# Attention units 3 to 6 of a two-block float32 forward pass: the wide product in halves

## The chip, the cores and the metric

One core of one Trainium2 chip runs the whole kernel. The metric is the device time in microseconds (us) of that core. TensorE multiplies (PE in the profile, its weight loads PEld), VectorE is DVE, ScalarE is ACT, GpSimd is POOL, and SyncE (SP) issues the weight DMAs.

## What is computed

The reference is a forward pass over 256 tokens of width 1024, in float32. The first block is two macaron layers (SwiGLU, gated linear attention or retention, SwiGLU, layer norms between them). The second block is one layer with three attention branches. The change stands in the second block's first projection, of which this matters here:

```python
proj = jnp.einsum('bsd,dc->bsc', x, w_in[layer])
(qa, ka, va, qi, ki, wi, qf, kf, vf, fg, qs, ks_, vs, gates) = jnp.split(proj, split_at, axis=-1)
o_a = _dsa_attention(heads(qa), heads(ka), heads(va),
                     qi.reshape(b, s, IDX_HEADS, IDX_DIM), ki, wi, slopes)
log_f = jax.nn.log_sigmoid((fg + b_forget[layer]).astype(jnp.float32))
o_b = _forgetting_attention(heads(qf), heads(kf), heads(vf), log_f)
o_c = _stick_breaking_attention(heads(qs), heads(ks_), heads(vs))
```

The first branch (`_dsa_attention`) scores every earlier token with 16 small index heads (`relu(qi . ki)` weighted by `wi`), keeps the 64 best keys of each query, and takes a softmax over these alone. The second adds the running sum of `log_f` to its logits.

## The kernel before

**Precision.** Every operand of a large product is split into a high part that TensorE's fast float32 format holds and a low part, the rest. A product is hi by hi, hi by lo and lo by hi, summed in PSUM. Weights come as tiles of 128x2048, one DMA each, in a ring of three slots (`RING = 3`). For tile m, ACT copies the high part (`split_hi`, L428) after the last use of tile m-3; DVE subtracts to get the low part (`split_lo`, L905); the DMA of tile m+3 waits for that subtraction.

**Units.** The second block's projection runs in units of 512 output columns, two weight tiles each. With n the first tile, unit u takes tiles n+2u and n+2u+1. Unit 0 gives the first branch's values, units 1 and 2 the index queries, 3 and 4 the first branch's queries and keys, 5 and 6 the second branch's, 7 its values, 8 and 9 the third branch's queries and keys, 10 its values. A unit's result goes to one of two pairs of PSUM banks, `pairs[0]` and `pairs[1]`. Semaphore `pair_free` counts how often a pair has been read out, `pair_count(u)` is the value that unit u brings it to, `ret_count` the same in an earlier stage. The other four banks, `acc`, take the small products of the attention itself.

**Three forms of a unit.** `tokens_unit` has the weights as the moving operand. `features_unit` has them as the stationary one: for each of 8 chunks of 128 rows and 4 blocks of 128 columns it issues three 256-column matmuls (`three`, L1574, L1577, L1578). One ACT copy (`part`, L678) reads the pair out, and the next unit writes the other pair meanwhile. `features_halves` (L1706, L1713) does two of the four blocks at a time. A 512-column matmul takes the high weights against the high and low activations side by side, and a 256-column one the low weights against the high activations. Half 0 goes through both tiles into one pair, half 1 again through both tiles into the other. Each pair then holds two parts, which have to be added: ACT copies one out (`against_lo_half`, L519) and DVE adds the other (`halves`, through `sum_half`, L997), which frees the pair. Half 0 signals `half_ready`; the tiles are released by half 1, the first one three quarters through the unit. In `before` the units 1, 2, 8 and 9 are halves, 3 to 6 are plain.

**Order.** Each engine's queue is written out by hand and runs in that order. `between={c: f}` puts small work f into TensorE's stream: ahead of chunk c in the plain forms; in the halves form the key is 2*(2*half + tile) ahead of the wide matmuls, and one more ahead of the narrow ones. The small work here is: `dots(p)`, index scores of pass p, whose relu is ACT's `relu_dots(p)` (L694) and whose weighting is DVE's `index_scores(p)` (L1297, L1299); `forget_sums`; `logits(0, g)`; `turn_p`, transposes of the probabilities (L2143 to L2145), copied out by `pt_copy` on ACT and DVE; `softmax_values`. On DVE, `pick_largest(tb, 4)` takes four rounds of eight maxima (L1307, L1308); four calls make up the choice of keys. `logits(0, g)` on DVE adds distances and takes row maxima (L1316 to L1330). `first_logits` on TensorE is `logits(0, 0)`; `third_logits` is `logits(0, 2)`, which waits for the row maxima of group 0 (`max_ready`), because it writes the same banks. After the exponentials (ACT, L707) and reciprocals (DVE, L1341), POOL scales the probabilities (L401) and `turn_p(0, ...)` waits for its last group.

Of the kernel before, what the change touches and what calls it, by code (L numbers as in the profile page):

```python
# [29 lines left out]
HEADS, HEAD_DIM = 8, 64  # L30
# [31 lines left out]
def build(nc, io):  # L62
    ctx = ExitStack()
    with ctx:
# [202 lines left out]

        wide = ["ffn0", "ffn1", "ffn2", "ret1", "ret2", "ret3", "ret4", "ffn3", "sec1", "sec2", "sec8", "sec9"]  # L270
        half_value = lambda what: wide.index(what) + 1
        copies_of = lambda what: 1 if what.startswith("ffn") else 2
        copied_value = lambda what, half: sum(copies_of(w) for w in wide[:wide.index(what)]) + half + 1
        ret_count = lambda u: 6 + u // 2
        pair_count = lambda u: 12 if u == 0 else (13 if u < 8 else 14) + u // 2

        block = ctx.enter_context(nc.Block())

# [129 lines left out]
        def _(act):  # L408
# [144 lines left out]
            n = N_GLA  # L553
# [118 lines left out]
            def part(u, out, scale=1.0, mid=None):  # L672

                split_hi(n + 2 * u + 3)
                if mid:
                    mid()
                act.wait_ge(weights_used, n + 2 * u + 2)
                nc.scalar.activation(out, pairs[u % 2], ACT.Copy, scale=scale).then_inc(pair_free[u % 2], 1)  # L678
# [11 lines left out]
            def relu_dots(p):  # L690
                act.wait_ge(dots_ready, p + 1)
                if p >= 2:
                    act.wait_ge(dots_used, p - 1)
                nc.scalar.activation(relu[:, p % 2, :].rearrange("p (b c) -> p b c", b=2),  # L694
                                     acc[:, 2 * (p % 2):2 * (p % 2) + 2, :], ACT.Relu).then_inc(relu_done, 1)
# [86 lines left out]
            halves(2, (pairs[1], pairs[0]), a_qi[:, 4:8, :], mid=lambda: relu_dots(0), late=lambda: relu_dots(1))  # L782
            split_hi(n + 8)
            relu_dots(2)
            part(3, as_pair(a_q[:, 0]), HEAD_DIM ** -0.5, mid=lambda: (relu_dots(3), relu_dots(4)))
            split_hi(n + 10)
            relu_dots(5)
            part(4, as_pair(a_k[:, 0]), mid=copy_sums)
            split_hi(n + 12)
            part(5, as_pair(a_q[:, 1]), HEAD_DIM ** -0.5)  # L790
            split_hi(n + 14)
            part(6, as_pair(a_k[:, 1]))
            split_hi(n + 16)
            softmax_exp(0, 0)
            part(7, a_v[:, 1], mid=lambda: softmax_exp(0, 1))
# [92 lines left out]
        def _(dve):  # L888
# [10 lines left out]
            def split_lo(n, i=0):  # L899

                if n >= N_TILES:
                    return
                s = slot_of(n)
                dve.wait_ge(hi_split, i * RING + (n + 1))
                nc.vector.tensor_tensor(w_lo[:, s, :], raw[:, s, :], w_hi[:, s, :].bitcast(F32),  # L905
                                        ALU.subtract).then_inc(lo_split, 1)
# [396 lines left out]
            def pick_largest(tb, rounds):  # L1303

                score = a_sc[:, 0, block_cols(tb)]
                for _ in range(rounds):
                    link(nc.vector.max(out=a_top[:, :], in_=score))  # L1307
                    link(nc.vector.match_replace(out=score, in_to_replace=a_top[:, :], in_values=score, imm_value=TAKEN))  # L1308
# [106 lines left out]
            for tb in range(TB):  # L1415
# [8 lines left out]
            index_scores(1)  # L1424
            split_lo(n + 8)
            index_scores(2)
            split_lo(n + 9)
            index_scores(3)
            index_scores(4)
            split_lo(n + 10)  # L1430
            index_scores(5)
            link(nc.vector.tensor_tensor(a_sc[:, 0, :], a_sc[:, 0, :], causal, ALU.add))
            dve.wait_ge(cT_copied, 1)
            nc.vector.scalar_tensor_tensor(out=a_cT[:, 1, :], in0=acc[0:HEAD_DIM + HEADS, 0, 0:TOK], scalar=-1.0,
                                           in1=a_cT[:, 0, :].bitcast(F32), op0=ALU.mult, op1=ALU.subtract).then_inc(cT_split, 1)
            split_lo(n + 11)
            pick_largest(1, 4)
            split_lo(n + 12)
            pick_largest(1, 4)
            split_lo(n + 13)  # L1440
            pick_largest(0, 4)
            split_lo(n + 14)
            pick_largest(0, 4)

            link(nc.vector.tensor_scalar(a_sc[:, 0, :], a_sc[:, 0, :], TAKEN, NEG, ALU.not_equal, ALU.mult))
            link(nc.vector.tensor_tensor(a_sc[:, 0, :], a_sc[:, 0, :], causal, ALU.min))
            split_lo(n + 15)
            logits(0, 0)
            split_lo(n + 16)
            logits(0, 1)  # L1450
# [116 lines left out]
        def _(pe):  # L1567
# [495 lines left out]
            def unit(u, kind, **between):  # L2063
                await_pair(u)
                kind(n + 2 * u, pairs[u % 2], **between)
# [160 lines left out]
            pe.wait_ge(wf_copied, 1)  # L2226
            pe.wait_ge(ki_doubled, 16)
            features_halves(n + 4, (pairs[1], pairs[0]), awaits(1, 12, 0, 13), "sec2", between={4: lambda: dots(0), 6: lambda: dots(1)})
            unit(3, features_unit, between={1: lambda: dots(2), 3: lambda: dots(3), 5: lambda: dots(4)})
            unit(4, features_unit, between={1: lambda: dots(5), 4: forget_sums})  # L2230
            unit(5, features_unit)

            def first_logits():
                pe.wait_ge(pick_copied, 1)
# [12 lines left out]
            def third_sums():  # L2247
                pe.wait_ge(max_ready, 3 + 1)
                key_sums(2)

            unit(6, features_unit, between={4: first_logits, 6: lambda: logits(0, 1)})
            unit(7, tokens_unit, between={4: third_logits})
            features_halves(n + 16, pairs, awaits(0, 16, 1, 16), "sec8")
            turn_p(0, range(0, 4))
            features_halves(n + 18, pairs, awaits(0, 17, 1, 17), "sec9", between={4: lambda: turn_p(0, range(4, 8))})
            unit(10, tokens_unit, between={0: lambda: softmax_values(0, 0), 2: lambda: softmax_values(0, 1),
                                           3: lambda: key_sums(0), 4: lambda: logits(1, 0), 5: second_sums,
                                           6: lambda: logits(1, 1)})
            merge_unit(0, between={1: third_sums, 2: lambda: logits(1, 2)})
# [176 lines left out]
```

## Time and profile before

| | us |
|---|---|
| median of 3 runs (1535.52 to 1535.70) | 1535.62 |
| the profiled execution's own time | 1535.63 |
| its span in the trace | 1533.8 |
| PE busy | 1525.2 |
| DVE busy | 966.8 |
| ACT busy | 754.6 |
| POOL busy | 130.8 |

1.83 us of the profiled execution lie outside the span. Busy time of PE overstates it: the records of matmuls overlap, so start-to-start times are the ones to read. The units 3 to 8 begin at 1094.67, 1110.03, 1124.11, 1135.63, 1149.71 and 1161.82 us of the span, unit 8 ends at 1172.97. In the timeline view the first column is the start, the second the duration (from the first start to the last end where a row merges several), in brackets the idle time ahead of it and what ended it.

### The profile page before, as it was taken

The numbers are of one execution on the slowest core, as the hardware profiler recorded it, in microseconds if no ns is written. First come the engines' busy times: TensorE is split into PE (matmuls) and PEld (weight loads), VectorE is DVE, ScalarE is ACT, GpSimd is POOL, SyncE is SP. The second block draws the span as 40 slices with busy tenths as digits, with TensorE's granted clock in tenths as the row PEclk, the third lists the DMA queues.
The fourth block names the chain that finished last, engine by engine and source line by source line (L and its number), as shares of the span: only waits on it lengthen the run. The fifth ranks groups of instructions, "written<-read, shape, count | busy, mean of one in ns | idle before, by whom it ended". The sixth has DMA issues, their size and how long they took to land.

```text
span 1533.8 us, 20565 instructions
## 1 busy us (share of the span) xinstructions
PE 1525.2 (99%) x8204; PEld 1301.6 (85%) x8204; DVE 966.8 (63%) x983; ACT 754.6 (49%) x723; POOL 130.8 (9%) x141
## 2 busy tenths in 40 slices
PE   9999999999999999999999999999999999999998
PEld 8888888788888888888878888888898788888886
DVE  6555676665557655577557665657686556775565
ACT  5454455554454545454335445445536556354442
POOL 1000020110002000024021200002002200020000
PEclk9999999999999999999999999999999999999999
DMA  7545564355544654556444465455444444455551
GB/s 308 196 189 184 198 220 165 110 220 195 193 187 165 234 200 169 200 211 220 172 165 162 149 238 192 168 215 215 173 155 148 144 159 165 165 197 202 193 188 71
DMA packets 42264, 283.71 MB, mean 185 GB/s; under 512 B 5088, under 2 KB 5536, under 8 KB 9552
## 3 DMA queue, kind: packets, MB, share of 16 engines
q1 hardware_dynamic: 38016, 270.55, 48.3%
q0 software_dynamic: 2368, 8.59, 1.6%
q10 hardware_dynamic: 1808, 3.55, 0.6%
q8 instruction: 54, 0.88, 0.2%
q14 instruction: 18, 0.15, 0.0%
HBM read 281.55 MB, written 1.05 MB: 184 GB/s over the span
## 4 chain that ended last, share of the span: by engine, by line
PE 99%; DVE 0%; ACT 0%; DVEq 0%; POOLq 0%; issue 0%; POOL 0%; ACTq 0%
PE psum L1679 20%; PE psum L1574 16%; PE psum L1577 16%; PE psum L1578 16%; PE psum L1683 11%; PE psum L1706 5%; PE psum L1713 2%; PE psum L1619 2%; PE psum L1606 2%; PE psum L1612 2%; PE psum L1586 1%; PE psum L2004 1%; PE psum L2133 0%; PE psum L2096 0%; PE psum L2154 0%; PE psum L1830 0%
## 5 line engine op out<-in xcount | busy, mean ns | idle before, releaser
L905 DVE TENSOR_TENSOR weights_lo<-weights_raw,weights_hi 128x2048 fp32r<-128x2048 f32 x247 | 569.7, 2318 | 324.6 <-ACT weights_hi L428 323.4
L428 ACT ACTIVATE weights_hi<-weights_raw 128x2048 fp32r<-128x2048 f32 (+1 forms) x254 | 479.5, 1890 | 297.0 <-PE psum L1578 140.3
L1679 PE MATMUL psum<-operand,weights_hi 128*128 128x512 f32 x1376 | 327.6, 390 | 0.0
L1679 PEld LDWEIGHTS psum<-operand,weights_hi 128*128 128x128 f32 x1376 | 255.3, 188 | 51.1
L1574 PE MATMUL psum<-weights_hi,hidden_hi 128*128 128x512 f32 x480 | 187.7, 391 | 0.0
L1577 PE MATMUL psum<-weights_lo,hidden_hi 128*128 128x512 f32 x480 | 187.6, 391 | 0.0
L1578 PE MATMUL psum<-weights_hi,hidden_lo 128*128 128x512 f32 x480 | 186.8, 389 | 0.0
L1683 PEld LDWEIGHTS psum<-operand,weights_lo 128*128 128x128 f32 x1376 | 176.4, 191 | 6.7
L1683 PE MATMUL psum<-operand,weights_lo 128*128 128x256 f32 x1376 | 178.5, 283 | 0.0
L1574 PE MATMUL psum<-weights_hi,operand 128*128 128x512 f32 x384 | 153.4, 399 | 0.0
L1577 PE MATMUL psum<-weights_lo,operand 128*128 128x512 f32 x384 | 150.0, 391 | 0.0
L1578 PE MATMUL psum<-weights_hi,operand 128*128 128x512 f32 x352 | 137.3, 390 | 0.0
L1578 PEld LDWEIGHTS psum<-weights_hi,hidden_lo 128*128 128x128 f32 x480 | 90.1, 188 | 19.0
L1574 PEld LDWEIGHTS psum<-weights_hi,hidden_hi 128*128 128x128 f32 x480 | 90.3, 188 | 17.5
L1577 PEld LDWEIGHTS psum<-weights_lo,hidden_hi 128*128 128x128 f32 x480 | 90.3, 188 | 17.0
L499 ACT ACTIVATE gate_up<-psum 128x512 f32<-128x512 f32 x72 | 39.1, 595 | 129.0 <-PE psum L1683 129.0
L322 POOL TENSOR_SCALAR ln_rstd<-variance 128x1 f32<-128x1 f32 x16 | 5.1, 317 | 1015.3 <-ACTq L450 1015.3
L1036 DVE TENSOR_TENSOR gate_up<-psum,gate_up 128x512 f32<-128x512 f32 x72 | 46.4, 687 | 68.0 <-ACT gate_up L499 68.0
L1574 PEld LDWEIGHTS psum<-weights_hi,operand 128*128 128x128 f32 x384 | 72.1, 188 | 17.5 <-issue 2.8
L1577 PEld LDWEIGHTS psum<-weights_lo,operand 128*128 128x128 f32 x384 | 72.2, 188 | 14.2 <-issue 0.5
L1706 PE MATMUL psum<-operand,weights_hi 128*128 128x512 f32 x320 | 80.5, 393 | 0.0
L1578 PEld LDWEIGHTS psum<-weights_hi,operand 128*128 128x128 f32 x352 | 66.1, 188 | 14.1
(295 smaller groups left out, 1836.1 us busy)
## 6 DMA issues: line engine op xcount, KB each, us to landing
weights_raw<-in_weights SPq DMA_DIRECT2D x254, 1024.0 KB, 4.8
ln_rows<-in_ln_rows POOLq DMA_DIRECT2D x16, 512.0 KB, 6.7
weights_raw<-in_weights SPq DMA_DIRECT2D x4, 512.0 KB, 6.6
normalised<-in_x SPq DMA_DIRECT2D x2, 512.0 KB, 6.2
ret_constants<-in_ret_constants ACTq DMA_DIRECT2D x1, 1024.0 KB, 7.4
out<-normalised SPq DMA_DIRECT2D x4, 256.0 KB, 2.0
gla_w_low<-in_gla_w_low ACTq DMA_DIRECT2D x1, 512.0 KB, 5.5
att_w_small<-in_att_w_small ACTq DMA_DIRECT2D x1, 512.0 KB, 5.6
```

The source lines that it names most:

```text
L428: nc.scalar.activation(w_hi[:, s, whole], raw[:, s, whole], ACT.Copy).then_inc(hi_split, 1)
L499: nc.scalar.activation(gate_up[:, at:at + 2, :], against_lo(banks), ACT.Copy).then_inc(against_lo_copied, 1)
L905: nc.vector.tensor_tensor(w_lo[:, s, :], raw[:, s, :], w_hi[:, s, :].bitcast(F32), ALU.subtract).then_inc(lo_split, 1)
L1036: nc.vector.tensor_tensor(gate_up[:, at:at + 2, :], against_hi(banks), gate_up[:, at:at + 2, :], ALU.add).then_inc(up_summed if at else ga ...
L1574: mm(out, a_hi, b_hi, start=start, stop=False, skip_group_check=True)
L1577: mm(out, a_hi, b_lo, start=False, stop=False, skip_group_check=True)
L1578: return mm(out, a_lo, b_hi, start=False, stop=stop, skip_group_check=True)
L1606: mm(out[:, tb, :], x_hi[:, c, t], w_hi[:, slot, cols], start=c == 0, stop=False, skip_group_check=True)
L1612: ins = mm(out[:, tb, :], x_lo[:, c, t], w_hi[:, slot, cols], start=False, stop=last and c == KC - 1, skip_group_check=True)
L1679: mm(banks[b // 2][:, b % 2, :], w_hi[:, slot, cols], x_both[:, c, :, :].rearrange("p a t -> p (a t)"), start=c == 0, stop=False, skip_gro ...
L1683: last = mm(banks[b // 2][:, b % 2, 0:TOK], w_lo[:, slot, cols], x_hi[:, c, :], start=False, stop=c == KC - 1, skip_group_check=True)
L1706: mm(banks[half][:, b, :], w_hi[:, slot, cols], x_both[:, c, :, :].rearrange("p a t -> p (a t)"), start=c == 0, stop=False, skip_group_che ...
```

## The change

Units 3 to 6 take the halves form. They enter the list `wide`, and `pair_count` rises by two from unit 1 on, as each halves unit reads out both pairs. On TensorE their small work keeps its keys. `sec8` and `sec9` wait for higher counts. The first `turn_p` moves from between units 8 and 9 into unit 9, key 2 (half 0, second tile); the second from key 4 to key 6 (half 1, second tile); the first `softmax_values` from chunk 0 to chunk 1 of unit 10. On ACT `part` becomes `halves`: two copies of 512 columns in the place of one of 1024, the first as soon as half 0 is done. On DVE eight additions (L997) come in, put among the splits, `index_scores` and `pick_largest`; and `split_lo(n + 11)` now stands ahead of `index_scores(5)`, the other splits two steps apart as before.

```diff
-        wide = [..., "ffn3", "sec1", "sec2", "sec8", "sec9"]
+        wide = [..., "ffn3", "sec1", "sec2", "sec3", "sec4", "sec5", "sec6", "sec8", "sec9"]
-        pair_count = lambda u: 12 if u == 0 else (13 if u < 8 else 14) + u // 2
+        pair_count = lambda u: 12 if u == 0 else (15 if u < 8 else 16) + u // 2
...
-            part(3, as_pair(a_q[:, 0]), HEAD_DIM ** -0.5, mid=lambda: (relu_dots(3), relu_dots(4)))
+            halves(3, (pairs[1], pairs[0]), a_q[:, 0], HEAD_DIM ** -0.5, mid=lambda: relu_dots(3), late=lambda: relu_dots(4))
             split_hi(n + 10)
             relu_dots(5)
-            part(4, as_pair(a_k[:, 0]), mid=copy_sums)
+            halves(4, (pairs[1], pairs[0]), a_k[:, 0], mid=copy_sums)
             split_hi(n + 12)
-            part(5, as_pair(a_q[:, 1]), HEAD_DIM ** -0.5)
+            halves(5, (pairs[1], pairs[0]), a_q[:, 1], HEAD_DIM ** -0.5)
             split_hi(n + 14)
-            part(6, as_pair(a_k[:, 1]))
+            halves(6, (pairs[1], pairs[0]), a_k[:, 1])
...
             index_scores(2)
+            halves(3, 0, a_q[:, 0], HEAD_DIM ** -0.5)
             split_lo(n + 9)
             index_scores(3)
+            halves(3, 1, a_q[:, 0], HEAD_DIM ** -0.5)
+            split_lo(n + 10)
             index_scores(4)
-            split_lo(n + 10)
+            halves(4, 0, a_k[:, 0])
+            split_lo(n + 11)
             index_scores(5)
...
-            split_lo(n + 11)
-            pick_largest(1, 4)
+            halves(4, 1, a_k[:, 0])
             split_lo(n + 12)
             pick_largest(1, 4)
+            halves(5, 0, a_q[:, 1], HEAD_DIM ** -0.5)
             split_lo(n + 13)
-            pick_largest(0, 4)
+            pick_largest(1, 4)
+            halves(5, 1, a_q[:, 1], HEAD_DIM ** -0.5)
             split_lo(n + 14)
             pick_largest(0, 4)
-
+            halves(6, 0, a_k[:, 1])
+            split_lo(n + 15)
+            pick_largest(0, 4)
             link(nc.vector.tensor_scalar(a_sc[:, 0, :], a_sc[:, 0, :], TAKEN, NEG, ALU.not_equal, ALU.mult))
             link(nc.vector.tensor_tensor(a_sc[:, 0, :], a_sc[:, 0, :], causal, ALU.min))
-            split_lo(n + 15)
+            halves(6, 1, a_k[:, 1])
             logits(0, 0)
...
-            unit(3, features_unit, between={1: lambda: dots(2), 3: lambda: dots(3), 5: lambda: dots(4)})
-            unit(4, features_unit, between={1: lambda: dots(5), 4: forget_sums})
-            unit(5, features_unit)
+            features_halves(n + 6, (pairs[1], pairs[0]), awaits(1, 13, 0, 14), "sec3", between={1: lambda: dots(2), 3: lambda: dots(3), 5: lambda: dots(4)})
+            features_halves(n + 8, (pairs[1], pairs[0]), awaits(1, 14, 0, 15), "sec4", between={1: lambda: dots(5), 4: forget_sums})
+            features_halves(n + 10, (pairs[1], pairs[0]), awaits(1, 15, 0, 16), "sec5")
...
-            unit(6, features_unit, between={4: first_logits, 6: lambda: logits(0, 1)})
+            features_halves(n + 12, (pairs[1], pairs[0]), awaits(1, 16, 0, 17), "sec6", between={4: first_logits, 6: lambda: logits(0, 1)})
             unit(7, tokens_unit, between={4: third_logits})
-            features_halves(n + 16, pairs, awaits(0, 16, 1, 16), "sec8")
-            turn_p(0, range(0, 4))
-            features_halves(n + 18, pairs, awaits(0, 17, 1, 17), "sec9", between={4: lambda: turn_p(0, range(4, 8))})
-            unit(10, tokens_unit, between={0: lambda: softmax_values(0, 0), 2: lambda: softmax_values(0, 1),
+            features_halves(n + 16, pairs, awaits(0, 18, 1, 18), "sec8")
+            features_halves(n + 18, pairs, awaits(0, 19, 1, 19), "sec9", between={2: lambda: turn_p(0, range(0, 4)), 6: lambda: turn_p(0, range(4, 8))})
+            unit(10, tokens_unit, between={1: lambda: softmax_values(0, 0), 2: lambda: softmax_values(0, 1),
```

## Rows read from the trace of the kernel before

**Rows 1.** The page: span, busy times, and the chain that ended last, by engine.

```profile
PE 1525.2 (99%) x8204; PEld 1301.6 (85%) x8204; DVE 966.8 (63%) x983; ACT 754.6 (49%) x723; POOL 130.8 (9%) x141
...
PE 99%; DVE 0%; ACT 0%; DVEq 0%; POOLq 0%; issue 0%; POOL 0%; ACTq 0%
```

**Rows 2.** The waits view, PE's only row: waiter, releaser, total, times, longest.

```profile
PE psum L1830 <- DVE squares L1059: 1.4, 1, 1.4
```

**Rows 3.** Stretches: length; PE, PEld, DVE, ACT, POOL busy; granted PE clock, DMA share.

```profile
0.00:1.45 1.45, 0.00 (x1) 0.00 (x1) 0.48 (x1) 0.26 (x1) 0.29 (x5) 1.00 0.00 0
...
1094.67:1110.03 15.36, 15.36 (x131) 14.09 (x130) 12.54 (x21) 7.17 (x6) 0.00 (x0) 1.00 0.45 155
1110.03:1124.11 14.08, 14.08 (x126) 13.82 (x126) 11.41 (x22) 5.99 (x6) 0.00 (x0) 1.00 0.37 138
1124.11:1135.63 11.52, 11.52 (x98) 11.52 (x98) 10.01 (x21) 4.74 (x3) 0.00 (x0) 1.00 0.44 173
1135.63:1149.71 14.08, 14.08 (x114) 13.06 (x114) 13.11 (x39) 4.74 (x3) 0.00 (x0) 1.00 0.55 176
...
1161.82:1172.97 11.15, 11.15 (x66) 9.83 (x65) 6.66 (x25) 8.31 (x20) 7.45 (x14) 1.00 0.49 182
```

**Rows 4.** Timeline of PE: halves in unit 2; third logits in unit 7.

```profile
1080.95 2.00 PE L1706 MATMUL psum<-operand,weights_hi 128*128 128x512 f32 x8
1082.79 1.12 PE L1713 MATMUL psum<-operand,weights_lo 128*128 128x256 f32 x8
1083.75 2.00 PE L1706 MATMUL psum<-operand,weights_hi 128*128 128x512 f32 x8
...
1155.15 1.16 PE L2133 MATMUL psum<-att_kT,att_qT 64*128 64x128 f32 x16
```

**Rows 5.** Timeline of ACT: a split and a copy-out, both in unit 1's half 1.

```profile
1078.42 1.92 ACT L428 ACTIVATE weights_hi<-weights_raw 128x2048 fp32r<-128x2048 f32 x1 [2.58 <-PE psum L1713]
1081.15 0.60 ACT L519 ACTIVATE att_qiT<-psum 128x512 f32<-128x512 f32 x1 [0.82 <-PE psum L1713]
```

**Rows 6.** Timeline of DVE: the work that stands between units 4 and 7.

```profile
1080.37 2.29 DVE L905 TENSOR_TENSOR weights_lo<-weights_raw,weights_hi 128x2048 fp32r<-128x2048 f32 x1 [3.62 <-ACT weights_hi L428]
...
1095.50 0.69 DVE L997 SCALAR_TENSOR_TENSOR att_qiT<-psum,att_qiT 128x512 f32<-128x512 f32 x1 [0.39 <-ACT att_qiT L519]
1096.10 2.04 DVE L1299 SCALAR_TENSOR_TENSOR att_score<-att_pT,att_wi_fg,att_score 128x256 f32<-128x256 f32 x4
...
1115.24 3.06 DVE L1299 SCALAR_TENSOR_TENSOR att_score<-att_pT,att_wi_fg,att_score 128x128 f32<-128x128 f32 x8
1118.45 0.56 DVE L1432 TENSOR_TENSOR att_score<-att_score,att_constants 128x384 f32<-128x384 f32 x1
1119.64 0.42 DVE L1434 SCALAR_TENSOR_TENSOR att_minus_cT<-psum,att_minus_cT 72x256 fp32r<-72x256 f32 x1 [0.64 <-ACT att_minus_cT L700]
...
1129.38 0.42 DVE L1307 MAX8 att_top<-att_score 128x8 f32<-128x256 f32 x1
...
1133.31 2.29 DVE L905 TENSOR_TENSOR weights_lo<-weights_raw,weights_hi 128x2048 fp32r<-128x2048 f32 x1
...
1140.90 0.29 DVE L1307 MAX8 att_top<-att_score 128x8 f32<-128x128 f32 x1
...
1143.76 0.36 DVE L1445 TENSOR_SCALAR att_score<-att_score 128x384 f32<-128x384 f32 x1
...
1144.75 2.29 DVE L905 TENSOR_TENSOR weights_lo<-weights_raw,weights_hi 128x2048 fp32r<-128x2048 f32 x1
...
1149.92 0.17 DVE L1330 TENSOR_SCALAR att_max<-att_max 128x4 f32<-128x4 f32 x1
1152.65 2.29 DVE L905 TENSOR_TENSOR weights_lo<-weights_raw,weights_hi 128x2048 fp32r<-128x2048 f32 x1 [2.56 <-ACT weights_hi L428]
```

**Rows 7.** Timeline of POOL: scaling of the first branch's probabilities, three groups.

```profile
1158.18 4.35 POOL L401 TENSOR_SCALAR att_p<-att_p,att_sum 128x256 f32<-128x256 f32 x4 [91.90 <-DVE att_sum L1341]
1164.86 6.73 POOL L401 TENSOR_SCALAR att_p<-att_p,att_sum 128x256 f32<-128x256 f32 x12 [2.33 <-DVE att_sum L1341]
```

More of the change, by code:

```diff
@@ L266, in build @@
         sig_of = lambda half, b: sig[3 if (half, b) == (1, 2) else b]
-        wide = ["ffn0", "ffn1", "ffn2", "ret1", "ret2", "ret3", "ret4", "ffn3", "sec1", "sec2", "sec8", "sec9"]
+        wide = ["ffn0", "ffn1", "ffn2", "ret1", "ret2", "ret3", "ret4", "ffn3", "sec1", "sec2", "sec3", "sec4", "sec5", "sec6", "sec8", "sec9"]
         half_value = lambda what: wide.index(what) + 1
@@ L1435, in _ @@
                                            in1=a_cT[:, 0, :].bitcast(F32), op0=ALU.mult, op1=ALU.subtract).then_inc(cT_split, 1)
-            split_lo(n + 11)
-            pick_largest(1, 4)
+            halves(4, 1, a_k[:, 0])
             split_lo(n + 12)
             pick_largest(1, 4)
+            halves(5, 0, a_q[:, 1], HEAD_DIM ** -0.5)
             split_lo(n + 13)
+            pick_largest(1, 4)
+            halves(5, 1, a_q[:, 1], HEAD_DIM ** -0.5)
+            split_lo(n + 14)
             pick_largest(0, 4)
-            split_lo(n + 14)
+            halves(6, 0, a_k[:, 1])
+            split_lo(n + 15)
             pick_largest(0, 4)
```

## The prediction

> **What bounds the kernel now.** The page comes first: PE is busy for 99% of the span and the chain that ended last runs through PE for 99% [rows 1]. Overlapping records can hide a short stop, so the waits view is next: PE waited once, 1.4 us in the opening [rows 2]. Then the stretches in which units 3 to 6 stand. Unit 5, which has nothing between its 96 matmuls, takes 11.52 us. Unit 3 has three passes of `dots` and takes 15.36, so one pass costs 1.28; units 4 and 6 have two pieces of small work and take 14.08, again 1.28 each [rows 3]. The times add up with nothing left over: TensorE never waits here, and only a shorter stream of TensorE gains. The question is whether the other engines still come in time, and for that the timelines of ACT and DVE are read [rows 5, 6]. The sum is made against the profiled execution's 1535.63 us, 0.01 from the median of 1535.62.
>
> **What TensorE saves.** A plain unit is 96 matmuls of 256 columns in 11.52 us, 0.120 each. Unit 8 is a halves unit without small work: 11.15 us [rows 3]. In unit 2, eight wide and eight narrow matmuls take 1083.75 - 1080.95 = 2.80 us, 1.84 of it the wide ones, 0.230 each [rows 4]. So a wide matmul costs 0.010 less than the two that it replaces, and a unit 11.52 - 11.15 = 0.37 less; four units 1.48 us, all on the path. I cost the moves of small work inside the stream at nothing: the same instructions run, and `dots` costs the same in plain units as between halves.
>
> For the spacing of matmuls the Trainium skill (TensorE: Matmul & The Clock Gate, Back-to-back issue gap) gives N/2.4 + 2.5 ns. By that a pair of 256 columns costs 218.4 ns against 215.8 for one of 512, which would save 0.08 us a unit. Units 3 and 4 would then end 0.5 us later than below and the queue of DVE, which decides from there, with them: 1540.6. The rows above show 0.120 and 0.230, so the sum goes by them.
>
> **What the other queues get.** ACT copies twice 512 columns at 0.60 each in the place of 1024 at once, at most 0.60 more a unit on an engine busy for less than half of these stretches [rows 3, 5]; free. SP's loads follow `split_lo`, and at 0.37 to 0.55 DMA share [rows 3] I cost them at nothing; were one late, TensorE would stop for the difference. DVE gets eight additions of 0.60 (start to next start; 0.69 to the end) [rows 6], 4.8 us. Its busy time in units 3 to 6 is 12.54 + 11.41 + 10.01 + 13.11 = 47.07 of 55.04 us [rows 3], so on the average there are 7.97 us for 4.8. But the change also makes its dates tighter. Before, the readout of a pair had a whole unit to happen, and was ACT's alone. Now half h of the next unit waits for DVE's addition of half h, which leaves one half-unit, 5.58 us, and `pick_largest` stands ahead of it in DVE's queue. And a tile's first slot is freed after three quarters of the unit, not after one half, so the splits start later. So I follow the queue.
>
> Steps on DVE, start to next start [rows 6]: an addition is 0.69 long and the next step starts 0.60 after it, an overlap of 0.09 in PSUM reads and 0.08 elsewhere; a split 2.29 - 0.08 = 2.21; `index_scores(5)` 1118.45 - 1115.24 = 3.21; the causal addition 0.56; the cT step 0.42 - 0.08 = 0.34; a long `pick_largest` 1133.31 - 1129.38 = 3.93, a short one 1143.76 - 1140.90 = 2.86; the two mask steps 1144.75 - 1143.76 = 0.99; the first logits, up to the end of the row maxima, 1149.92 + 0.17 - 1144.75 less a split, 3.13. Handovers: TensorE to ACT 0.26 (unit 1's third quarter ends at 1080.95 - 2.79 = 1078.16, ACT starts at 1078.42), ACT to DVE 0.03 (1078.42 + 1.92 to 1080.37) [rows 4 to 6]. No row shows TensorE waiting for DVE at speed; the nearest are these two, so it is 0.03 to 0.26, and I take 0.15, the middle, as neither is nearer.
>
> - TensorE ends unit 3 at 1094.67 + 14.99 = 1109.66. It frees tile n+8 in unit 4 after three quarters and two pieces of small work: 1109.66 + 8.37 + 2.56 = 1120.59. Unit 4 ends at 1123.37; half 1 of unit 5 is due at 1128.95.
> - ACT splits tile n+11: 1120.59 + 0.26 + 1.92 = 1122.77. DVE, idle until then with `index_scores(5)` ready behind the split, starts at 1122.80: 2.21, 3.21, 0.56, 0.34 lead to 1129.12, and the addition `halves(4, 1)` ends at 1129.81. TensorE goes on at 1129.96: **stop 1, 1.01 us**.
> - DVE goes on from 1129.72: split, long pick, 1135.86; `halves(5, 0)` ends at 1136.55. Unit 6 was due at 1129.96 + 5.58 = 1135.54 and starts at 1136.70: **stop 2, 1.16**.
> - From 1136.46: split, long pick, 1142.60; `halves(5, 1)` ends at 1143.29. Half 1 of unit 6, due at 1142.28, starts at 1143.44: **stop 3, 1.16**.
> - From 1143.20: split, short pick, `halves(6, 0)`, 1148.87. The split of n+15 has to wait for ACT, which waits for TensorE's third quarter of unit 6, 1143.44 + 1.28 + 2.79 = 1147.51; it starts at 1149.72. Split, short pick, mask, `halves(6, 1)`, logits: 2.21 + 2.86 + 0.99 + 0.60 + 3.13 lead to 1159.51 for the first row maxima. TensorE ends unit 6 at 1151.58, and reaches the third logits 5.44 us into unit 7 (before: 1155.15 - 1149.71 [rows 3, 4]), at 1157.02. It goes on at 1159.66: **stop 4, 2.64**.
>
> Stops 5.97, savings 1.48: **+4.49 us**. Cross-check: the third logits move from 1155.15 to 1159.66, 4.51 later. Behind them no date is tight that was not before.
>
> **The moved transposes.** POOL's last group ended at 1164.86 + 6.73 = 1171.59 [rows 7], 1.38 ahead of the transposes at 1172.97, and 21.50 behind the maxima of 1150.09 [rows 6]. Within these DVE idled 2.56 for a split of ACT's [rows 6], which is now done before the maxima. So POOL ends between 1159.51 + 18.94 = 1178.45 and 1181.01; nearest is the lower, as that split is in time. Unit 8 ends at 1159.66 + 17.82 = 1177.48: in the old place TensorE would stop for 1.0 or more. In the new one, a quarter unit on, 1180.27, it waits 0 to 0.7; I take 0. The second group of transposes and the values move by as much or stay, with the same instructions, and cost nothing.
>
> **Forecast: 1535.63 + 4.49 = 1540.1 us.** Both ends of the handover count twice (stops 3 and 4), -0.24 to +0.22; gaps between some 30 linked DVE steps and the transposes' wait widen it to 1539.5 to 1540.9.
>
> **Rivals.**
> - *DVE keeps its dates* (not slower). The averages speak for it: 4.8 us of additions into 7.97 of idle time. If no stop comes, 1535.63 - 1.48 = 1534.15, within 0.2%. It decides at half 1 of unit 5: were the addition `halves(4, 1)` done by 1128.95 in place of 1129.81, and each later link 1 us shorter. Against it: by the hand count the idle time lies ahead of the splits of n+9 and n+11, which wait for tiles that TensorE frees late, and is lost to the steps queued behind them. In part: the loss falls under 0.2% (3.07 us) if the chain to the maxima is 1.4 us shorter than my 36.7.
> - *The probabilities come late* (slower still). POOL's last group at 1181.0 or beyond, then the DVE and ACT copies of the transposes, ahead of ACT's split of n+21: 0.7 to 2 us on top, 1540.9 to 1542.1. For it: POOL works 6.73 us on the last two groups. Against: the 1.8 us of slack above.
> - *TensorE's clock falls in the stops.* The granted clock is 1.00, the 2.4 GHz level, in every stretch, also in the opening with its 1.45 us of idleness [rows 3]. The longest stop here is 2.64 us, longer than any that a row shows. If the following half unit ran at 1.2 GHz, twice its 5.58 us, the time were 1545.7. The Trainium skill (TensorE: Matmul & The Clock Gate, Loop structure matters more than you think) says that a wait that leaves PE idle for long drops the clock; no row here shows that.
> - *The wide product saves nothing here.* Then unit 4's third quarter ends 0.65 us later, and the queue of DVE sets the rest as above: 1540.8. Against it stand unit 8 and unit 5.
>
> **Chances.** Forecast 0.74; DVE keeps its dates 0.13 (half of that in full, half in part, up to 1538.7); late probabilities 0.08; clock 0.02; no saving 0.03. All but the first rival lie over 0.2% slower (about what a measurement of this kernel can tell from no change): slower 0.87; the first rival is same, 0.12; faster 0.01 is left for what I don't see, since the parts can save 1.48 us at most. The range leaves out the full first rival, the clock and the tail: 1538.5 to 1542.0.
>
> **What would show it.** After: L1706 has 448 matmuls, plain 256-column triples are gone. PE idle time appears in the waits view, ended by DVE L997, at half 1 of unit 5, unit 6's start and its half 1, about 1.1 us each, and by DVE L1330 ahead of L2133 in unit 7, about 2.6. DVE runs without idle time of note from the split of n+11 to the maxima. The first transposes follow the first tile of unit 9 without a stop. Unit 5 spans 11.15 plus stop 1. It would be wrong if PE shows no wait for DVE, or if L2143 waits for POOL.

## The result and the profile after

The changed kernel takes 1541.61 us (median of 6 runs, 1541.43 to 1542.15) against 1535.66 (6 runs, 1535.47 to 1536.12) in the same comparison: 5.95 us or 0.39% slower, ratio 1.0039, 95% interval 1.0029 to 1.0049. The forecast was 1540.1, in a range from 1538.5 to 1542.0. The sign was right and the time lies in the range; the loss was forecast as 4.49 and measured as 5.95. The profiled execution took 1541.75 us, with a span of 1539.9; it runs 0.23 us behind the one of before from the opening on (unit 3 starts at 1094.90 in place of 1094.67), which belongs to no part of the change.

The waits view of after, PE's rows (waiter, releaser, total, times, longest). Before there was only the one of the opening [rows 2].

```profile
PE psum L2140 <- DVE att_max L1330: 2.4, 1, 2.4
PE psum L1837 <- DVE squares L1059: 1.4, 1, 1.4
PE psum L2140 <- DVE att_qT L997: 0.9, 1, 0.9
PE psum L1713 <- DVE att_qT L997: 0.9, 1, 0.9
PE psum L1713 <- DVE att_kT L997: 0.8, 1, 0.8
```

There are four new waits, all for DVE: three for an addition (L997) and one for the first row maxima (L1330). The timeline of PE in after shows their places, and what comes behind the last. (The changed kernel is seven lines longer: what was L1706 and L1713 there is L1713 and L1720 here, L1574 is L1581, L2133 is L2140 and L2143 is L2150; in the reordered kernels some lines stand one earlier.)

```profile
1130.09 2.12 PE L1713 MATMUL psum<-operand,weights_hi 128*128 128x512 f32 x8 [0.75 <-DVE att_kT L997]
...
1136.82 2.11 PE L1713 MATMUL psum<-operand,weights_hi 128*128 128x512 f32 x8 [0.88 <-DVE att_qT L997]
...
1143.56 1.13 PE L2140 MATMUL psum<-att_kT,att_qT 64*128 64x256 f32 x8 [0.89 <-DVE att_qT L997]
...
1156.84 0.39 PE L1585 MATMUL psum<-weights_hi,operand 128*128 128x512 f32 x1
1159.68 1.55 PE L2140 MATMUL psum<-att_kT,att_qT 64*128 64x128 f32 x16 [2.45 <-DVE att_max L1330]
...
1162.60 0.63 PE L1581 MATMUL psum<-weights_hi,operand 128*128 128x512 f32 x1
1163.03 0.63 PE L1584 MATMUL psum<-weights_lo,operand 128*128 128x512 f32 x1
...
1164.51 0.39 PE L1581 MATMUL psum<-weights_hi,operand 128*128 128x512 f32 x1
1164.74 0.39 PE L1584 MATMUL psum<-weights_lo,operand 128*128 128x512 f32 x1
```

Start to start, the 512-column matmul at 1156.84 should be followed after 0.23 us and is followed after 2.84: the stop is 2.61. Then look at the spacing: 0.43 us a matmul at 1162.60, 0.23 at 1164.51. The stretches of after say why (columns as in [rows 3]):

```profile
1094.90:1109.86 14.96, 14.96 (x99) 11.94 (x98) 9.22 (x17) 7.49 (x7) 0.00 (x0) 1.00 0.39 140
1109.86:1123.59 13.73, 13.73 (x94) 11.99 (x93) 9.57 (x13) 6.59 (x8) 0.00 (x0) 1.00 0.46 154
1123.59:1136.82 13.23, 11.60 (x66) 9.85 (x64) 12.52 (x27) 5.75 (x6) 0.00 (x0) 1.00 0.42 160
1136.82:1151.60 14.78, 13.89 (x80) 11.42 (x81) 13.67 (x29) 4.08 (x3) 0.00 (x0) 1.00 0.40 142
...
1159.68:1163.81 4.13, 4.13 (x22) 3.39 (x23) 4.10 (x10) 3.76 (x9) 0.00 (x0) 0.59 0.20 42
1163.81:1167.94 4.13, 4.13 (x20) 3.38 (x19) 4.09 (x13) 2.08 (x8) 2.98 (x2) 1.00 0.52 218
```

Units 3 and 4 are 0.40 and 0.35 shorter than before [rows 3]. The stops follow. And behind the last one the granted clock is 0.59 over 4.13 us, most of it the 1.2 GHz level. From the third logits to the end of unit 7 TensorE takes 1167.94 - 1159.68 = 8.26 us; before it took 1161.82 - 1155.15 = 6.67 [rows 3, 4]. The fall costs 1.59 us. The sum from the trace: 4.53 - 0.23 = 4.30 us up to the third logits, 1.59 behind them, 5.89. With the 0.23 of the opening that is 6.12, all of the difference between the two profiled executions (1541.75 and 1535.63).

DVE's timeline in after, the chain that was counted from [rows 6]:

```profile
1123.00 2.29 DVE L905 TENSOR_TENSOR weights_lo<-weights_raw,weights_hi 128x2048 fp32r<-128x2048 f32 x1 [3.63 <-ACT weights_hi L428]
...
1129.36 0.68 DVE L997 SCALAR_TENSOR_TENSOR att_kT<-psum,att_kT 128x512 f32<-128x512 f32 x1
...
1136.08 0.69 DVE L997 SCALAR_TENSOR_TENSOR att_qT<-psum,att_qT 128x512 f32<-128x512 f32 x1
...
1142.82 0.69 DVE L997 SCALAR_TENSOR_TENSOR att_qT<-psum,att_qT 128x512 f32<-128x512 f32 x1
...
1149.74 2.29 DVE L905 TENSOR_TENSOR weights_lo<-weights_raw,weights_hi 128x2048 fp32r<-128x2048 f32 x1 [0.56 <-ACT weights_hi L428]
...
1159.36 0.17 DVE L1330 TENSOR_SCALAR att_max<-att_max 128x4 f32<-128x4 f32 x1
```

DVE idles 3.63 us ahead of the split of tile n+11 and then only 0.56 up to the maxima, which end at 1159.53. The hand count had 1159.51, but without the late start of 0.23: the chain itself was 0.21 us quicker than counted.

### The profile page after: what moved, and what is told of

Its sections match the earlier page's. It is cut to its first block, busy times and chain, and to the rows that moved or that the text cites. A ratio compares the mean times of both kernels' runs of the same rounds, so it can differ in the third digit from the quotient of the medians.

```text
span 1539.9 us, 20321 instructions
## 1 busy us (share of the span) xinstructions
PE 1526.4 (99%) x8076; PEld 1296.4 (84%) x8076; DVE 972.0 (63%) x991; ACT 755.7 (49%) x727; POOL 130.7 (8%) x141
## 3 DMA queue, kind: packets, MB, share of 16 engines
HBM read 281.55 MB, written 1.05 MB: 184 GB/s over the span
## 4 chain that ended last, share of the span: by engine, by line
PE 97%; DVE 2%; ACT 0%; issue 0%; DVEq 0%; POOLq 0%; POOL 0%; ACTq 0%
PE psum L1686 20%; PE psum L1581 15%; PE psum L1584 15%; PE psum L1585 15%; PE psum L1690 11%; PE psum L1713 6%; PE psum L1720 3%; PE psum L1626 2%; PE psum L1613 2%; PE psum L1619 2%; PE psum L1593 1%; PE psum L2011 1%; DVE weights_lo L905 1%; PE psum L2103 0%; PE psum L2161 0%; PE psum L2140 0%
## 5 line engine op out<-in xcount | busy, mean ns | idle before, releaser
L1686 PE MATMUL psum<-operand,weights_hi 128*128 128x512 f32 x1376 | 327.6, 391 | 0.0
L1686 PEld LDWEIGHTS psum<-operand,weights_hi 128*128 128x128 f32 x1376 | 255.4, 188 | 51.0
L1581 PE MATMUL psum<-weights_hi,hidden_hi 128*128 128x512 f32 x480 | 187.9, 391 | 0.0
L1581 PE MATMUL psum<-weights_hi,operand 128*128 128x512 f32 x384 | 154.1, 401 | 0.0
L1713 PE MATMUL psum<-operand,weights_hi 128*128 128x512 f32 x448 | 113.1, 395 | 1.6 <-DVE att_qT L997 0.9
L1581 PEld LDWEIGHTS psum<-weights_hi,hidden_hi 128*128 128x128 f32 x480 | 90.3, 188 | 17.4
L1713 PEld LDWEIGHTS psum<-operand,weights_hi 128*128 128x128 f32 x448 | 80.9, 189 | 18.1 <-issue 1.3
L1581 PEld LDWEIGHTS psum<-weights_hi,operand 128*128 128x128 f32 x384 | 72.6, 189 | 17.7 <-issue 3.0
```

What stands on the lines that cost most here:

```text
L1581: mm(out, a_hi, b_hi, start=start, stop=False, skip_group_check=True)
L1686: mm(banks[b // 2][:, b % 2, :], w_hi[:, slot, cols], x_both[:, c, :, :].rearrange("p a t -> p (a t)"), start=c == 0, stop=False, skip_gro ...
L1713: mm(banks[half][:, b, :], w_hi[:, slot, cols], x_both[:, c, :, :].rearrange("p a t -> p (a t)"), start=c == 0, stop=False, skip_group_che ...
```

## The experiments

Theory: DVE's queue between units 4 and 7 stops TensorE, and the longest stop takes the clock along. The rivals: the slow matmuls have another cause; DVE's sum of work and not its order decides; the halves form saves nothing; the moves cost or are needed. All edits are of the changed kernel unless said otherwise. The kernel before ran beside each: 1535.75 beside the third logits two chunks later, the two with fewer rounds and the transposes put back; 1535.62 beside the moves alone and the splits around the scaling; 1535.70 beside the others.

### The third logits two chunks later

```diff
-            unit(7, tokens_unit, between={4: third_logits})
+            unit(7, tokens_unit, between={6: third_logits})
```

> The changed kernel with TensorE's third logits two chunks later in unit 7 (key 6 in place of 4), nothing else. Theory A (the stop of 2.6 us ahead of the third logits is followed by about 4 us at the 1.2 GHz level, 1.6 us dear, because TensorE stood still): TensorE reaches the logits at 1159.8, when the row maxima are there, so there is no stop in unit 7, the granted clock stays 1.00, and the 2.6 and the 1.6 both go; but unit 8 then ends early and half 0 of unit 9 waits some 1.4 us for DVE's addition of unit 8, which stands behind the third group's reciprocals. Total by the hand-worked queues: 1541.6 - 1.6 - 1.2 = 1538.9 us. Theory B (the slow matmuls have another cause, for instance PSUM traffic of DVE and ACT right behind the first maxima): the slow stretch stays at the same place in time, 1540.4 us.

Measured: 1544.3 us (four executions, 1543.54 to 1545.26), ratio 1.0053 (1.0037 to 1.0070). Both theories missed the time, but the trace separates them. The third logits stand at 1160.15 there, without a stop, and the stretches around them have 1.00 granted:

```profile
1150.00:1160.00 10.00, 10.00 (x49) 8.26 (x47) 9.58 (x30) 3.85 (x4) 0.00 (x0) 1.00 0.33 116
1160.00:1170.00 10.00, 10.00 (x63) 8.54 (x63) 9.90 (x27) 8.54 (x19) 4.36 (x4) 1.00 0.40 143
```

DVE and ACT do the work behind the first maxima at the same time as in the changed kernel, so theory B is out. New is a stop further on. Its PE timeline, then POOL's and DVE's:

```profile
1176.23 2.11 PE L1713 MATMUL psum<-operand,weights_hi 128*128 128x512 f32 x8 [0.83 <-DVE att_qT L997]
...
1182.70 0.48 PE L2150 MATMUL psum<-constants,att_p 128*128 128x128 f32 x1 [3.41 <-POOL att_p L401]
```

```profile
1171.91 10.73 POOL L401 TENSOR_SCALAR att_p<-att_p,att_sum 128x256 f32<-128x256 f32 x12 [2.33 <-DVE att_sum L1341]
```

```profile
1171.74 2.26 DVE L905 TENSOR_TENSOR weights_lo<-weights_raw,weights_hi 128x2048 fp32r<-128x2048 f32 x1
...
1177.29 2.31 DVE L905 TENSOR_TENSOR weights_lo<-weights_raw,weights_hi 128x2048 fp32r<-128x2048 f32 x1 [1.11 <-ACT weights_hi L428]
...
1180.13 2.28 DVE L905 TENSOR_TENSOR weights_lo<-weights_raw,weights_hi 128x2048 fp32r<-128x2048 f32 x1
```

TensorE waits 3.41 us for POOL, and from 1182.70 to 1187.00 its granted clock is 0.50. POOL's last twelve instructions take 10.73 us; in the changed kernel it was 6.58, before 6.73 [rows 7]. Three splits of DVE lie over them here, one there: as TensorE came earlier (unit 8 ends at 1175.24, in the changed kernel at 1179.08), ACT's and DVE's splits of the next tiles did too.

### The split behind the scaling

The edit above, and:

```diff
             halves(8, 0, a_q[:, 0], HEAD_DIM ** -0.5)
+            dve.wait_ge(p_ready, 3)
             split_lo(n + 19)
```

> The run with the third logits at key 6, and in addition DVE's split of tile n+19 waits until POOL has scaled the third group's probabilities. In that run (1544.3 us) POOL's last twelve instructions took 10.73 us against 6.58 in the changed kernel, and two splits of DVE lay over them; TensorE waited 3.4 us for POOL and its clock fell after that. Theory (a POOL instruction that starts while DVE is in a split stands until the split is over, 2.1 us each): with the splits behind it POOL ends about 4 us earlier, at 1178.5, ahead of the transposes, and neither the wait nor the clock's fall comes: 1539.0 us. Rival (POOL is slow for another reason, and DVE's queue is only made later by the wait): 1544.3 or more.

Measured: 1538.66 us (1538.41 to 1539.13), ratio 1.0020 (1.0010 to 1.0029): 5.6 us less, by a wait more. POOL and DVE:

```profile
1171.49 6.57 POOL L401 TENSOR_SCALAR att_p<-att_p,att_sum 128x256 f32<-128x256 f32 x12 [2.33 <-DVE att_sum L1341]
```

```profile
1178.10 2.29 DVE L905 TENSOR_TENSOR weights_lo<-weights_raw,weights_hi 128x2048 fp32r<-128x2048 f32 x1 [2.34 <-POOL att_p L401]
```

POOL is back at 6.57, 4.16 less for two splits, 2.1 each. No wait for POOL is left, and 1.00 is granted throughout the attention. So an instruction of POOL that meets a split of DVE stands for about the split's length: the longest of POOL's instructions here takes 2.54 us, their median is 0.47. The Trainium skill (SBUF — State Buffer, Who interferes with whom) says that a DVE `tensor_tensor` with both inputs in SBUF and a GpSimd instruction that reads SBUF exclude each other, the later one waiting in full; the trace agrees, with 2.1 us each, and in these runs it was POOL that stood: DVE's splits took 2.26 to 2.39 us throughout the attention. Against the changed kernel, 4.2 us were taken off in unit 7 (stop 4 and the clock), and the stop ahead of unit 9, about 1.0 from start to start, came in: 3.2, where the medians differ by 2.95 and the profiled executions by 3.16.

### One round less, half the rounds

```diff
-            pick_largest(0, 4)
+            pick_largest(0, 3)
             link(nc.vector.tensor_scalar(a_sc[:, 0, :], a_sc[:, 0, :], TAKEN, NEG, ALU.not_equal, ALU.mult))
```

> The changed kernel with the last call of pick_largest cut from four rounds to three; it chooses 56 keys in place of 64 for the first 128 queries, so that part of the computation is left out. DVE's queue is 0.71 us shorter ahead of the row maxima, and the stop in unit 7 is about 1.9 us in place of 2.6. If the clock falls all the same: 1541.6 - 0.7 = 1540.9 us and a granted clock of about 0.6 for 4 us. If a stop of 1.9 us is too short for that: 1539.3 us and 1.00 throughout. Theory B as in the first run: 1540.9 and slow matmuls.

Measured: 1539.6 us, ratio 1.0028 (1.0018 to 1.0038), and the ten executions are of two kinds: six at 1539.18 to 1539.89, four at 1540.86 to 1541.27. These are the two forecasts, 1539.3 and 1540.9. The profiled execution is of the first kind: a wait of 1.73 us ahead of the third logits and 1.00 granted. That the four others had the clock fall is inferred from their time.

```diff
-            pick_largest(1, 4)
+            pick_largest(1, 2)
...
-            pick_largest(0, 4)
+            pick_largest(0, 2)
```

(each of these lines stands twice and is changed twice)

> The changed kernel with all four calls of pick_largest cut to two rounds (half of the keys are chosen; that part of the computation is left out). 6.8 us of DVE's queue go. Theory: the queue of DVE between unit 4 and unit 7 is all that stops TensorE; with it shortened all four stops and the clock's fall go and the saving of the halves form is left: 1535.6 - 1.5 = 1534.1 us. Rival (the halves form itself costs TensorE more than counted, or other stops stand behind): 1535.6 or more.

Measured: 1536.77 us, ratio 1.0007 (0.9997 to 1.0016). The forecast of 1534.1 was missed and the rival's "other stops" came true. The stops at unit 6's start and its half 1 are gone; two are left, in PE's waits view:

```profile
PE psum L2140 <- DVE att_max L1330: 1.0, 1, 1.0
...
PE psum L1713 <- DVE att_kT L997: 0.8, 1, 0.8
```

The second stands ahead of every `pick_largest`, so it could not go with them, which the expectation overlooked; for the first the maxima came at 1155.66, still later than TensorE. With these, from start to start, 1535.75 - 1.48 + 0.9 + 1.2 = 1536.4, 0.4 under the time. That fits the saving of the halves form; the clock held (1.00 in the profile).

### The transposes back, and the moves alone

```diff
-            features_halves(n + 18, pairs, awaits(0, 19, 1, 19), "sec9", between={2: lambda: turn_p(0, range(0, 4)), 6: lambda: turn_p(0, range(4, 8))})
-            unit(10, tokens_unit, between={1: lambda: softmax_values(0, 0), 2: lambda: softmax_values(0, 1),
+            turn_p(0, range(0, 4))
+            features_halves(n + 18, pairs, awaits(0, 19, 1, 19), "sec9", between={4: lambda: turn_p(0, range(4, 8))})
+            unit(10, tokens_unit, between={0: lambda: softmax_values(0, 0), 2: lambda: softmax_values(0, 1),
```

> The changed kernel with the transposes and values of the first branch back where they were in the kernel before. POOL's last group ended at 1178.21, unit 8 at 1179.08, so the transposes would find their operand in either place: 1541.6 us, within 0.2. Rival (the move was needed, or it costs something itself): 1 us more, or some tenths less.

Measured: 1541.83 us (five runs: four at 1541.48 to 1542.14, one at 1545.48), ratio 1.0038 (1.0024 to 1.0053). The median is as expected, and the profiled execution is the odd one. Up to the end of unit 8 it runs the same program as the changed kernel, with the same four waits (0.75, 0.88, 0.88 and 2.45 us), and yet in it the clock held behind stop 4:

```profile
1159.27:1163.00 3.73, 3.73 (x28) 3.15 (x29) 3.70 (x6) 3.73 (x9) 0.00 (x0) 1.00 0.15 24
```

TensorE then was early at the transposes (unit 8 ended at 1177.08), a second split lay over POOL's work (8.64 us in place of 6.58), TensorE waited 2.69 us for POOL, and its clock fell there, to 0.50 over 4.27 us:

```profile
1179.93 0.48 PE L2150 MATMUL psum<-constants,att_p 128*128 128x128 f32 x1 [2.69 <-POOL att_p L401]
```

So the move buys nothing where the clock falls in unit 7. Where it holds, it covers a late POOL: in the profiled execution with one round less, which has the move, POOL's last group took 8.60 us and ended at 1179.33, 2.7 us behind unit 8's end at 1176.60, and the transposes began at 1179.39 without a wait.

The same moves in the kernel before, alone:

```diff
-            turn_p(0, range(0, 4))
-            features_halves(n + 18, pairs, awaits(0, 17, 1, 17), "sec9", between={4: lambda: turn_p(0, range(4, 8))})
-            unit(10, tokens_unit, between={0: lambda: softmax_values(0, 0), 2: lambda: softmax_values(0, 1),
+            features_halves(n + 18, pairs, awaits(0, 17, 1, 17), "sec9", between={2: lambda: turn_p(0, range(0, 4)), 6: lambda: turn_p(0, range(4, 8))})
+            unit(10, tokens_unit, between={1: lambda: softmax_values(0, 0), 2: lambda: softmax_values(0, 1),
```

> The kernel before with the moves of the transposes and the values alone, units 3 to 6 in their plain form. Theory: the same instructions at other places of a stream that never waits, 1535.7 us, within 0.3. Rival (the moved small work costs by its place, or ACT's split of tile n+21 comes late behind the second copies): 1 us more.

Measured: 1535.65 us against 1535.62, ratio 1.0000 (0.9991 to 1.0010). The moves cost nothing.

### The scores ahead of the split

```diff
-            split_lo(n + 11)
             index_scores(5)
...
                                            in1=a_cT[:, 0, :].bitcast(F32), op0=ALU.mult, op1=ALU.subtract).then_inc(cT_split, 1)
+            split_lo(n + 11)
             halves(4, 1, a_k[:, 0])
```

> The changed kernel with DVE's split of tile n+11 behind index_scores(5), the causal addition and the cT step instead of ahead of them, nothing else. Theory (DVE stood idle for 3.6 us ahead of that split, with work that was ready queued behind it): the chain runs 2.5 us earlier, the stops at half 1 of unit 5 and at unit 6's start go, the one in unit 6 shrinks to 0.8, the one ahead of the third logits stays at 2.6 and the clock falls behind it: 1535.6 + 1.7 + 1.6 = 1538.9 us (1537.4 where the clock holds). Rival (DVE's sum of work decides, not its order): no change, 1541.6.

Measured: 1539.46 us, ratio 1.0021 (1.0011 to 1.0031); three executions at 1537.54 to 1537.62, five at 1539.22 to 1539.65, one at 1540.81. One line's place is worth 2.2 us (1541.61 to 1539.46), so the rival, by which only DVE's sum of work counts, is out. In the profiled execution:

```profile
1141.03 1.13 PE L2140 MATMUL psum<-att_kT,att_qT 64*128 64x256 f32 x8 [0.56 <-DVE att_qT L997]
...
1157.14 1.16 PE L2140 MATMUL psum<-att_kT,att_qT 64*128 64x128 f32 x16 [2.44 <-DVE att_max L1330]
```

Two stops are left, as counted (0.72 us from start to start for 0.8, 2.6 for 2.6), and from 1157.14 to 1161.30 the granted clock is 0.67.

### The queues reordered

Four edits on top of the last one:

```diff
+            halves(5, 1, a_q[:, 1], HEAD_DIM ** -0.5)
             pick_largest(1, 4)
-            halves(5, 1, a_q[:, 1], HEAD_DIM ** -0.5)
...
-            softmax_exp(0, 2)
-            halves(8, pairs, a_q[:, 0], HEAD_DIM ** -0.5)
+            halves(8, pairs, a_q[:, 0], HEAD_DIM ** -0.5, mid=lambda: softmax_exp(0, 2))
...
+            halves(8, 0, a_q[:, 0], HEAD_DIM ** -0.5)
             split_lo(n + 18)
             inverse_sums(0, 2)
-            halves(8, 0, a_q[:, 0], HEAD_DIM ** -0.5)
...
-            unit(7, tokens_unit, between={4: third_logits})
+            unit(7, tokens_unit, between={7: third_logits})
```

The first `turn_p` also goes to key 4 of unit 9.

> The changed kernel with its queues reordered: the split of tile n+11 behind index_scores(5); the addition of unit 5's half 1 ahead of the second pick_largest; the third logits at key 7 of unit 7; ACT's exponentials of the third group behind the copy of unit 8's half 0, and DVE's addition of that half ahead of the third reciprocals; the first transposes at key 4 of unit 9. By the hand-worked queues TensorE never stops, the clock stays at 1.00 and only the saving of the halves form is left: 1535.6 - 1.5 = 1534.1 us, faster than both kernels. Rival (the halves form doesn't save, or POOL's scaling, delayed by DVE's splits, stops the transposes): 1535.6 or more.

Measured: 1537.09 us (1536.45 to 1538.14), ratio 1.0010 (1.0000 to 1.0019). The rival's second half came true. No stop for DVE is left in PE's waits, but one for POOL:

```profile
PE psum L2149 <- POOL att_p L401: 2.0, 1, 2.0
```

POOL's twelve instructions take 10.92 us, with splits at 1169.33, 1173.83 and 1176.65 over them.

The same with the third logits back at key 4:

> The reordered kernel of the next run, but with the third logits at key 4 of unit 7 as in the changed kernel. By the hand-worked queues one stop is left, 2.6 us ahead of the third logits. If the clock falls behind it: 1535.6 + 0.9 + 1.6 = 1538.1 us; if it holds, 1536.5. Against the next run, the stop and the clock should cost 4.2 us together.

Measured: 1537.80 us, ratio 1.0015 (1.0005 to 1.0024), again of two kinds: five executions at 1536.86 to 1537.06, five at 1538.55 to 1539.19. The profiled one, of the first kind, has one wait that the kernel before has not, 2.45 us for the maxima, and 1.00 granted behind it:

```profile
1156.44:1160.60 4.16, 4.16 (x29) 3.52 (x30) 4.13 (x10) 3.78 (x9) 0.00 (x0) 1.00 0.22 45
```

The first kind is 0.4 above its forecast (1536.5), the second 0.8 (1538.1). That a wait of 2.45 us left the clock alone here and took it down in the changed kernel says that the length alone doesn't decide; and as one and the same program did both (the transposes put back, above), neither does the order of the kernel. The comparison of this run with the one above does not give the 4.2 us expected, as the stop for POOL has taken the place of the other.

### The splits around the scaling

In the reordered kernel:

```diff
             logits(0, 2)
+            split_lo(n + 18)
             inverse_sums(0, 1)
             halves(8, 0, a_q[:, 0], HEAD_DIM ** -0.5)
-            split_lo(n + 18)
             inverse_sums(0, 2)
             split_lo(n + 19)
             halves(8, 1, a_q[:, 0], HEAD_DIM ** -0.5)
+            dve.wait_ge(p_ready, 3)
             split_lo(n + 20)
```

> The reordered kernel (1537.1 us), whose one stop left was 2.0 us ahead of the first transposes, for POOL, with three splits of DVE over POOL's last twelve instructions (10.92 us). Here DVE's split of tile n+18 comes ahead of the second group's reciprocals, so that POOL's group starts behind it, and the split of n+20 waits until POOL has scaled the third group; only the split of n+19 can still lie over POOL's work. Theory (each overlapped split holds POOL for 2.1 us): POOL needs 6.4 us instead of 10.9 from a start 2.2 us later, ends 2.3 us earlier, and TensorE doesn't stop: 1537.1 - 2.0 = 1535.1 us, and with the start of the profiled execution as usual 1534.5; faster than before by a hair (0 to 1.3 us). Rival (POOL's time is not set by the splits): 1537 or more.

Measured: 1534.69 us (11 runs, 1534.34 to 1535.07) against 1535.62 (1535.44 to 1536.34), ratio 0.9993, 95% interval 0.9984 to 1.0002. POOL takes 6.65 us, and PE's waits view has the opening's row alone:

```profile
1170.48 6.65 POOL L401 TENSOR_SCALAR att_p<-att_p,att_sum 128x256 f32<-128x256 f32 x12 [4.53 <-DVE att_sum L1340]
```

With no stop left, the saving can be read by itself: units 3 to 6 run from 1094.66 to 1148.23, 53.57 us in place of 55.04, 1.47 less where 1.48 was counted. The run is 6.9 us faster than the changed kernel. It is 0.9 us under the kernel before, and each of its executions is under each of that one's, but the interval includes no change, so that it beats it is likely and not shown.

## Why the prediction was right, and where it was not

- **The time**: right in sign, and 1541.61 lies in the stated 1538.5 to 1542.0, but not in the 1539.5 to 1540.9 that the working gives for its sum. The range was said to leave out the clock, and the clock's fall is what brought the time to where it is; that the range holds it is in part luck. Up to the third logits, where the clock had no share, 4.49 us were counted and 4.30 came.
- **What bounds the kernel**: right. With no waits TensorE's stream is the time, and waits add to it one for one, with the clock's fall on top where it comes.
- **The saving**: 0.37 a unit counted, 0.40 and 0.35 measured for units 3 and 4, and 1.47 for all four where nothing stops TensorE ("The splits around the scaling"). The spacing formula of the Trainium skill (TensorE: Matmul & The Clock Gate, Back-to-back issue gap) would have given 0.08 a unit. The page calls it that of an isolated matmul; in this stream, where weights are loaded for every matmul, the measurement decides against it.
- **DVE's queue**: right in place and size. Stops counted at 1.01, 1.16, 1.16 and 2.64; start to start the trace of after has 0.92, 1.03, 1.05 and 2.61. The handover from DVE to TensorE was taken as 0.15 and is 0.05 at the additions (1129.36 + 0.68 to 1130.09) and 0.15 at the maxima (1159.53 to 1159.68). The rival that DVE keeps its dates, which the average idle time spoke for, is out: that idle time did lie ahead of the split of n+11, and taking `index_scores(5)` ahead of it gave 2.2 us back.
- **The clock**: the step that failed. The row of 1.00 in the opening, with its 1.45 us of idleness [rows 3], was read as a sign that 2.64 us would pass, and the rival got 0.02. It came, in all six executions by their times. Its price was guessed from a half unit at 1.2 GHz, 5.6 us, and is 1.59. With the chance turned round and the price right, the forecast would have been 1541.7. The Trainium skill (TensorE: Matmul & The Clock Gate, Loop structure matters more than you think) warns of a drop behind a long wait; the trace agrees, with the fall behind 2.45 us.
- **POOL**: 1178.45 forecast for the end of its last group, 1178.21 measured, and no wait of the transposes (from 1181.88 on), in part by luck. The count took POOL's 6.73 us [rows 7] as its own work; it holds 2.1 us of standing behind DVE's split of n+18, as does every such span here. Without the clock's fall, TensorE brings the next split earlier and POOL's end later, as the profiled execution with the transposes put back shows (1179.88).
- **The moves**: nothing counted, 0.03 us measured in the kernel before, far inside the noise.

What stays open: why the clock fell behind a wait of 2.45 us in some executions and held in others, and how it went in the executions of the changed kernel that were not profiled; their times, 1541.4 to 1542.2, all fit the fall. Several experiments ended 0.3 to 0.8 us above their count. Part of that lies ahead of the change: in the profiled executions unit 3 begins between 1094.51 and 1095.31 us, the latest in the reordered kernel. The rest I did not trace.

## What to carry to other kernels

An engine's average idle time says little about new work in its queue. Ask where in the queue the idle time lies, what ready work stands behind the wait that makes it, and which date the new work has to meet: going from one readout a unit to two parts halved the time to the date, and three stops of 1 us came of it. A stop of TensorE has two prices, its length and the clock behind it, and the second may come by chance; small work that waits should stand as late in the stream as its consumers allow, but a stop taken out brings the next date forward, and the first run here got slower by it (1544.3 us). Where GpSimd has a deadline, count the DVE splits that can fall over it.

## What the runs showed of the hardware

- Behind waits of 2.44 to 3.41 us TensorE's granted clock fell in some executions, in others not: 0.59 over 4.13 us behind 2.45 and 0.67 over 4.16 us behind 2.44, but 1.00 behind 2.45 in two profiles; 0.50 over 4.3 us behind 2.69 and behind 3.41. Behind waits of 0.56 to 2.00 us it was 1.00 in every profile. Of the ten executions of the kernel whose profile shows a 1.73 us wait, four are 1.8 us longer than the others; that their clock fell is inferred.
- A POOL instruction that meets a DVE subtraction with two inputs in SBUF stands until it is over: twelve instructions took 6.57 to 6.76 us with one split over them, 8.60 to 8.66 with two, and 10.73 and 10.92 with three, 2.1 more for each.
- A late TensorE can hide a late POOL: with the transposes in their old place, the four executions in which the clock fell in unit 7, by their times, took 1541.5 to 1542.1 us; the profiled one, in which it held there, waited 2.69 us for POOL and took 1545.48.
